# Output projection of a hybrid encoder layer: seven block products for eight, weight sums formed ahead, routing products set between dense ones

## What is computed

```python
h = rms_norm(x, norm1_g); proj = h @ w_in              # latents, z gate, delta-net inputs
mla_out = mla_mixer(...)                               # 8 heads of 128
gdn_out = gdn_mixer(...)                               # 8 heads of 128
x = x + jnp.concatenate([mla_out, gdn_out], axis=-1) @ w_o      # (768, 2048) @ (2048, 2048)
x = x + ec_moe(rms_norm(x, norm2_g), w_router, w_gate, w_up, w_down)
# ec_moe: affinities = softmax(xt @ w_router); each of the 16 experts takes its top
# 2*T/16 tokens of a set (32 of the prompt, 64 of the sample), SwiGLU of width 1024, added back
```

## Time and profile before

| | |
|---|---|
| median of 3 runs | 3069.76 us |
| profiled execution | 3071.65 us |
| its span (first to last instruction) | 3069.8 us |
| TensorE busy | 2891.6 us |
| mean granted TensorE clock | 0.976 of full |
| bytes moved | 561 MB, mean 183 GB/s |
| latents end / projection begins / last dense product ends / experts begin | 319.7 / 1625.2 / 1947.2 / 1966.6 us |

### The profile page before, as it was taken

One profiled execution on the slowest core, in us unless ns is written; L12 is line 12 of the kernel. 1 busy time (PEld: TensorE's weight loads), 2 busy tenths in 40 slices (PEclk: granted clock), 3 DMA queues, 4 the chain that ended last, 5 costly groups with the idle time before them and its releaser, 6 DMA issues. The chain is left out here.

```text
span 3069.8 us, 45507 instructions
## 1 busy us (share of the span) xinstructions
PE 2891.6 (94%) x19449; PEld 1451.7 (47%) x19449; DVE 890.9 (29%) x1613; ACT 512.7 (17%) x1333; POOL 409.8 (13%) x400
## 2 busy tenths in 40 slices
PE   8999999999999999998899999799999999999997
PEld 4544455555676666665564456333332232322232
DVE  1000344421764664675761022300000000000000
ACT  4110355412213213214111001100000000000000
POOL 0000111104114214215210000000110000011001
PEclk9999999999999999998999999899999999999998
DMA  5120200030211211103205113799999999999996
GB/s 184 55 73 21 68 28 28 11 118 28 56 53 38 56 42 49 56 15 118 72 22 212 55 55 155 289 404 397 386 390 381 395 395 394 393 394 387 391 396 250
DMA packets 140611, 561.01 MB, mean 183 GB/s; under 512 B 15216, under 2 KB 47816, under 8 KB 87240
## 3 DMA queue, kind: packets, MB, share of 16 engines
q1 hardware_dynamic: 131527, 534.08, 45.1%
q0 software_dynamic: 8960, 25.17, 3.9%
HBM read 524.25 MB, written 34.96 MB: 182 GB/s over the span
## 5 line engine op out<-in xcount | busy, mean ns | idle before, releaser
L2398 PE MATMUL psum<-wbuf,xeT 128*32 128x512 f32 x3120 | 356.8, 610 | 35.2 <-DMA wbuf<-in_w_up 32.3
L1222 PE MATMUL psum<-xT,wbuf 128*128 128x512 f32 x720 | 337.6, 606 | 0.3 <-PEq L612 0.3
L2398 PE MATMUL psum<-xT,xeT 128*32 128x512 f32 x3024 | 330.1, 592 | 0.0
L1992 PE MATMUL psum<-wbuf,xT 128*128 128x512 f32 x656 | 288.4, 601 | 1.0 <-PEq L1147 1.0
L460 PE MATMUL psum<-wbuf,xT 128*128 128x512 f32 (+1 forms) x704 | 281.1, 559 | 0.9 <-DVE xT L380 0.9
L2398 PEld LDWEIGHTS psum<-wbuf,xeT 128*32 128x32 f32 x3120 | 101.6, 113 | 283.6 <-issue 229.7
L2398 PEld LDWEIGHTS psum<-xT,xeT 128*32 128x32 f32 x3024 | 98.1, 110 | 226.4 <-issue 222.5
L1992 PEld LDWEIGHTS psum<-wbuf,xT 128*128 128x128 f32 x656 | 126.8, 195 | 157.6 <-issue 157.6
L460 PEld LDWEIGHTS psum<-wbuf,xT 128*128 128x128 f32 x704 | 133.4, 191 | 139.1 <-issue 120.0
L2481 DVE COPY hT<-psum 128x384 f32<-128x384 f32 x16 | 8.9, 557 | 646.9 <-PE psum L2381 646.9
L1222 PEld LDWEIGHTS psum<-xT,wbuf 128*128 128x128 f32 x720 | 132.1, 193 | 125.5 <-issue 120.5
(11 more groups left out here) (299 smaller groups left out, 3060.0 us busy)
## 6 DMA issues: line engine op xcount, KB each, us to landing
xT<-in_w_down SPq DMA_DIRECT2D x66, 1024.0 KB, 25.4
wbuf<-in_w_gate SPq DMA_DIRECT2D x65, 1024.0 KB, 20.1
wbuf<-in_w_up SPq DMA_DIRECT2D x65, 1024.0 KB, 23.5
xT<-in_w_gate SPq DMA_DIRECT2D x63, 1024.0 KB, 18.6
xT<-in_w_up SPq DMA_DIRECT2D x63, 1024.0 KB, 21.0
wbuf<-in_w_down SPq DMA_DIRECT2D x62, 1024.0 KB, 25.3
wbuf<-in_w_in SPq DMA_DIRECT2D x14, 2048.0 KB, 9.2
wbuf<-in_w_o SPq DMA_DIRECT2D x6, 4096.0 KB, 14.9
```

Source lines behind the costliest of these rows:

```text
L1222: last = nc.tensor.matmul(ps[:, b, 0:SS_], wg[:, m % 2, d, h * P:(h + 1) * P], k.xT[:, d, SP_:T], start=(d == 0), stop=(d == KD - 1))
L1992: last = nc.tensor.matmul(ps[:, u % 3, :], mixT[:, q, t * P:(t + 1) * P], wo[:, j % 2, q, :], start=(q == q0), stop=(q == 2 * H - 1))
L2398: last = nc.tensor.matmul(ps[32 * j:32 * j + 32, g, :].rearrange("p (x n) -> p x n", x=2), xeT[:, q, 32 * g:32 * g + 32], m[:, :, kk, 256 ...
```

## The change

**Seven products for eight.** The tiles are taken in pairs (even, odd) = (2, 3), (4, 5), (0, 1). The left matrix of a pair is [[E_l, E_h], [O_l, O_h]] (E and O: rows of the even and odd tile; l and h: heads 0 to 7 and 8 to 15), `w_o` is [[W_ll, W_lr], [W_hl, W_hr]] (low and high heads, left and right 1024 columns). With D = E_l - O_l, S2 = O_h - D, S1 = E_l + S2, S4 = E_h - S2 and the weight sums T1 = W_lr - W_ll, T3 = W_hr - W_lr, T2 = T3 + W_ll, N4 = W_hl - T2, seven products (p = 1: E_l W_ll, 2: E_h W_hl, 3: S4 W_hr, 4: O_h N4, 5: S1 T1, 6: S2 T2, 7: D T3), each of 8 heads for two halves j of 512 columns, give the four output blocks by additions. That is 3 x 7 x 2 x 8 = 336 products of 128 x 512 in place of 384. p = 1 and heads 0 to 6 of the first two units of p = 7 are made in deltanet.

**Weight sums in latents.** SP loads all four quarters of `w_o` in 32 steps of 128 partitions x 4 x 256 elements, VectorE combines each in three operations, and SP stores the four sums to `weight_sums`, 16 MB each way. 14 steps lie among the kv latents, 18 among the z slices.

**Routing between dense products.** A group of four transposes, or of four router products, follows each second dense product of a unit, in place of all 16 between two units.

```diff
@@ latents, SP @@
+                def comb_load(u):
+                    q, j, half = u // 4, (u // 2) % 2, u % 2
+                    if u >= 2:
+                        sp.wait_ge(s_cs[u % 2], 16 * (u // 2))
+                    c0 = 512 * j + 256 * half
+                    src = a["w_o"][0].rearrange("(g q p) (h c) -> g q p h c", g=2, p=P, h=2)[:, q, :, :, c0:c0 + 256]
+                    for g in range(2):
+                        sp.dma_start(comb[:, u % 2, 2 * g:2 * g + 2], src[g]).then_inc(s_cl[u % 2], 16)
+
+                def comb_store(lo, hi):
+                    for u in range(lo, hi):
+                        q, j, half = u // 4, (u // 2) % 2, u % 2
+                        c0 = 512 * q + 256 * half
+                        sp.wait_ge(s_comb, u + 1)
+                        sp.dma_start(k.wt[:, j, :, c0:c0 + 256].rearrange("m p c -> p m c"), comb[:, u % 2]).then_inc(s_cs[u % 2], 16)
+                        if 1 <= u < COMBOS - 1:
+                            comb_load(u + 1)
...
-                for g in range(1, 4):
-                    load_w(g)
+                load_w(1)
+                load_w(2)
+                comb_load(0)
+                comb_load(1)
+                comb_store(0, 11)
+                load_w(3)
                 sp.dma_start(k.wq[:], a["w_q_b"][0].rearrange("(p k) n -> p k n", k=4)[:, :, 0:2 * QH]).then_inc(k.s_wa, 16)
                 sp.dma_start(k.wkv[:], a["w_kv_b"][0].rearrange("(p k) n -> p k n", k=2)[:, :, 0:2 * (NOPE + VH)]).then_inc(k.s_wa, 16)
+                comb_store(11, 14)
                 sp.wait_ge(s_gv, 6)
...
+                    if half == 0:
+                        comb_store(14, 24)
+                    else:
+                        comb_store(24, COMBOS)
                     sp.wait_ge(s_z, NT * half + nt)
...
+                for x in range(2):
+                    sp.wait_ge(s_cs[x], 16 * COMBOS // 2)
@@ latents, VectorE @@
+                def combine(lo, hi):
+                    for u in range(lo, hi):
+                        w = comb[:, u % 2]
+                        dve.wait_ge(s_cl[u % 2], 32 * (u // 2 + 1))
+                        odd = w.rearrange("p (g h) c -> p g h c", h=2)[:, :, 1]
+                        st.done(nc.vector.tensor_tensor(w[:, 0:2], odd, w[:, 0:2], ALU.subtract))
+                        st.settle()
+                        st.done(nc.vector.tensor_tensor(w[:, 3], w[:, 3], w[:, 0], ALU.subtract))
+                        st.settle()
+                        nc.vector.tensor_tensor(w[:, 2], w[:, 2], w[:, 3], ALU.subtract).then_inc(s_comb, 1)
...
                 for u in range(NT - 1, 2 * NT):
                     store_latent(u)
+                    combine(2 * (u - NT + 1), 2 * (u - NT + 1) + 2)
...
                     nc.vector.tensor_tensor(o, o, bcast(gng[:], 1, 4), ALU.mult).then_inc(s_z, 1)
+                    if v < 9:
+                        combine(14 + 2 * v, 16 + 2 * v)
@@ deltanet, SP (last pair of heads) @@
+                        for j in range(2):
+                            sp.dma_start(k.slot[j], weight_half(a, 0, 0, j)).then_inc(k.s_wo[j], 16)
                         sp.wait_ge(s_out, i * 16)
                         sp.dma_start(k.mixT[:, H:2 * H - 2], k.mix[H:2 * H - 2].rearrange("h p t -> p h t")).then_inc(k.s_mix, 16)
-                        sp.dma_start(k.wo[:, 0], a["w_o"][0].rearrange("(k p) n -> p k n", p=P)[:, :, 0:512]).then_inc(k.s_wo[0], 16)
-                        sp.wait_ge(s_silu, HP * NC)
-                        for o, t in enumerate(PARTS):
-                            sp.dma_start(part[o], k.x_rows(t)[:, 0:512]).then_inc(s_px, 16)
...
-                for o in range(len(PARTS)):
+                sp.wait_ge(s_pp, N_PART)
+                sp.dma_start(k.slot[1], k.wt[T3, 1].rearrange("p (q n) -> p q n", q=H)).then_inc(k.s_wo[1], 16)
+                for o in range(N_PART):
                     sp.wait_ge(s_pa, o + 1)
                     sp.dma_start(k.part[o], part[o]).then_inc(s_out, 16)
@@ deltanet, GpSimd @@
+                        if r == 1 and i + 1 == HP:
+                            pool.wait_ge(k.s_mix, 32)
+                            for even, odd in PAIRS:
+                                o = k.mixT[:, 0:H, odd * P:(odd + 1) * P]
+                                nc.gpsimd.tensor_tensor(o, k.mixT[:, 0:H, even * P:(even + 1) * P], o, ALU.subtract).then_inc(s_convv, 1)
@@ output_and_route @@
-    ORDER = [2, 3, 4, 5, 0, 1]
+    ORDER = [3, 5, 2, 4, 0, 1]
+    PRODUCTS = [(p, j, i) for p in (7, 6, 5, 3, 4, 2) for j in range(2) for i in range(2)]
+    UNIT = [u // 2 for u in range(24)] + [10, 11] + list(range(12, 22))
+    PRODUCTS += [(p, j, 2) for p in (2, 6, 5, 3, 7, 4) for j in range(2)]
...
+    TURN = {20: 0, 21: 1, 24: 2, 25: 3, 33: 4}
+    ROUTE = {22: 0, 23: 1, 26: 2, 27: 3, 34: 4}
+    AFFINITY = {24: 0, 25: 1, 28: 2, 29: 3, 35: 4}
@@ output_and_route, SP @@
+                def load_w(v):
+                    u = UNIT.index(v)
+                    p, j, _ = PRODUCTS[u]
+                    if v >= 3:
+                        sp.wait_ge(s_acc, last_use[v - 3] + 1)
...
+                    sp.dma_start(k.slot[v % 3], src).then_inc(s_w[v % 3], 16)
...
+                sp.wait_ge(k.s_gdn, rows_to)
+                for t in ORDER[0:2]:
+                    sp.dma_start(x2[:, t, :], k.x_rows(t)).then_inc(k.s_gdn, 16)
+                load_w(2)
+                for t in ORDER[2:4]:
+                    sp.dma_start(x2[:, t, :], k.x_rows(t)).then_inc(s_x, 16)
+                sp.dma_start(part, k.part.rearrange("o p n -> p o n")).then_inc(k.s_mix, 16)
+                for t in ORDER[4:6]:
+                    sp.dma_start(x2[:, t, :], k.x_rows(t)).then_inc(s_x, 16)
...
+                for v in range(3, NV):
+                    load_w(v)
+                    if v == 12:
+                        rows_out(0)
+                        rows_out(1)
...
@@ output_and_route, TensorE @@
+                    for q in range(NEAR if u < 2 else 0, H):
...
+                        last = nc.tensor.matmul(ps[:, u % 3, :], left, k.slot[v % 3][:, q, :], start=(q == 0), stop=(q == H - 1))
...
+                        if q % 2 and u in TURN:
+                            transposes(TURN[u], q // 2)
+                        if q % 2 and u in ROUTE:
+                            router(ROUTE[u], q // 2)
+                        if q % 2 and q < H - 1 and u == NU - 1:
+                            last_transposes(q // 2)
```

More of the change, by code:

```diff
@@ L47, with weight_half @@
 SECOND = 8
-PARTS = (2, 3, 4, 5)
-PART_HEADS = 2 * H - 2
+PAIRS = ((2, 3), (4, 5), (0, 1))
+T1, T3, N4, T2 = range(4)
+COMBOS = 32
+N_PART = 6
+PART_STEPS = N_PART * H
+NEAR = H - 1
+def weight_half(a, low, right, j):
+    return a["w_o"][0].rearrange("(g q p) n -> g p q n", g=2, p=P)[low, :, :, 1024 * right + 512 * j:1024 * right + 512 * j + 512]
 def shape_constants():
@@ L167, in latents @@
     k.s_gdn = k.sem("deltanet_stored")
-    k.part = nc.dram_tensor("output_part", [len(PARTS), P, 512], F32).ap()
+    k.part = nc.dram_tensor("output_part", [N_PART, P, 512], F32).ap()
+    k.wt = nc.dram_tensor("weight_sums", [4, 2, P, H * 512], F32).ap()
+    k.slot = [k.wbuf[:, v // 2, H * (v % 2):H * (v % 2) + H, :] for v in range(4)]
     k.s_ring = [k.sem(f"unit_loaded{q}") for q in range(6)]
+    k.ring_base = [16 * COMBOS] * 2 + [8 * COMBOS] * 2 + [0] * 2
     k.s_act, k.act_steps = k.sem("scalar_step"), 0
@@ L1131, in deltanet @@
         s_vec = sem("deltanet_vector_step")
-        part = [(pre, y)[o // 3][:].rearrange("p b n -> p (b n)")[:, 512 * (o % 3):512 * (o % 3) + 512] for o in range(len(PARTS))]
+        part = [(pre, y)[o // 3][:].rearrange("p b n -> p (b n)")[:, 512 * (o % 3):512 * (o % 3) + 512] for o in range(N_PART)]
         w_d = a["w_in"][0].rearrange("(p k) n -> p k n", k=KD)
@@ L1760, in _ @@
                                 convolve(i + 1, 1, [lv + 1])
+                            if not more and r == 0 and lv == 5:
+                                copy_part(0)
+                            if not more and r == 1 and lv == LV:
+                                copy_part(2)
                         if r < 2:
@@ L1771, in _ @@
                     if not more:
-                        add_part(2)
+                        copy_part(5)
                     output(i)
-                    if not more:
-                        add_part(3)
                     if more:
@@ new lines, in transposes, with router @@
+                def transposes(o, b):
+                    if b == 0:
+                        pe.wait_ge(s_xn, o + 1)
+                    if o:
+                        pe.wait_ge((s_td, s_ta)[b % 2], 2 * o - 1 + b // 2)
+                    for j in range(4):
+                        m = 4 * b + j
+                        last = nc.tensor.transpose(ps[:, 3 + b, j * P:(j + 1) * P], xn[:, o % 2, m * P:(m + 1) * P], k.ident)
+                    last.then_inc(s_tp, 1)
+                def router(o, b):
```

(40 more changed lines are left out.)

296 lines of the change are left out of this document (162 added, 134 removed).

## The result

The changed kernel takes 3086.2 us (median of 4 runs, 3084.07 to 3087.41), the kernel before 3069.43 us beside it: ratio 1.0055, 95% interval 1.0042 to 1.0068. It is **slower by 17 us**; 3052 had been forecast, with a range of 3028 to 3076. The profiled execution took 3084.07 us; its span is 3082.3, 12.5 us more than the 3069.8 before.

The account below looks back on a forecast made before the run. The experts' weight stream sets their length, so time saved or lost before them counts in full. Projection -48.2, DeltaNet +0.7 and latents +30.3 sum to -17.2 us: 3052 us against the median 3069.76, range 3028 to 3076.

Parts of the forecast that it names:

- Weight sums in the latents: Latents: 32 load, combine, store steps form one serial chain; the stage ends at 350 against 319.7, +30 us.
- L: Period of one weight-sum step in the latents: 6.6 us, low bound 5.7, high bound 8.3.
- 185 + 25L: Time in us at which the latents end, given the sums' step period; 350 was forecast.
- detour behind step 10: Latents: SP issues z weights, wq and wkv (5.4 MB, 15 us), so step 12 comes 15.7 us after step 11.
- TensorE ahead of its cumulative sum: Latents: the cumulative sum, at 210.71 before, runs at 221, +10 us, behind VectorE's late gate arithmetic.
- Rival B: Latents: every load waits behind a store; slower from a period of 7.55 us, 3095 us at 8.3; chance 0.13.
- 25L - 182: Whole kernel's net change in us by the sums' step period; crosses zero at 7.3 us.
- Rival A: Latents: the sums hide, period 5.9 us or less; net -35 to -40, 3030 to 3035 us; chance 0.14.
- C: Projection: starved by weight loads of 12 us rather than 8; +26 us, net +9 or about -1; chance 0.06.
- D: Routing: the clock falls in spite of interleaving; +10 us, net -7, 3063 us; chance 0.08.
- Projection: Output projection with routing: products -46.3, routing -9.9, start +6, small waits +2; 321.8 to 273.6 us, -48.2.
- Routing: Projection: interleaving with dense products keeps the clock full, 38.0 to 28.1 us, -9.9; bounds 0 and -12.

Follow-up runs that it names:

- experiment 5: Changed kernel without the stores of the weight sums; combinations stay, the projection reads plain quarters of the weights: 3029.53 us.
- experiment 6: Changed kernel with each tile's four groups of transposes, or of router products, together behind a unit's last dense product: 3089.04 us.
- experiment 7: Kernel of experiment 6 with router products directly ahead of the next tile's transposes at three of four places: 3095.16 us, ratio 1.0084.
- experiment 2: Changed kernel with SP issuing the load of step u+1 ahead of its wait for step u's combination: 3040.88 us.
- experiment 3: Changed kernel with four buffers for the sums in place of two, three loads ahead: 3025.98 us.
- experiment 1: Changed kernel without the weight sums in the latents; the projection loads quarters of w_o of the same size instead: 3027.7 us.
- experiment 8: Four-buffer kernel with the projection's fourth and fifth weight loads issued ahead of router weights, gain and two late x tiles: 3013.74 us.

## Why the prediction was wrong, step by step

- **Weight sums in the latents: the step that failed**, in its term L. The mechanism was the forecast's: one serial chain, its three operations, SP's loads behind its stores. L was put at 6.6 us; it is 7.56. The term of the sum that was mis-sized is the moving of the store's and the load's 1.05 MB "behind each other at 350 GB/s, 3.0 us": the windows show 5.0 us, 1.5 for the store and 3.5 for the load. The 1.95 us put around it for first byte and completion are about 1.0, which hides half of the error. The load by itself was no surprise: without the store it costs 4.0 us from signal to landing (experiment 5), and the prediction's two bounds have 4.1 and 3.95 for it. It is the store ahead of it that adds 1.96, where 6.6 left 1.0.
- **Where the 350 GB/s came from**: a row that is mostly a 2 MB transfer. It held a warning: where its 1 MB store ends and the load begins stand three slices of 0.75 us at 243, 191 and 277 GB/s, 0.5 MB in some 2.2 us. The prediction took them for a dip of 0.5 us. To a load of 2 MB they are little, to one of 0.5 MB nearly all; that they are the same slowness as the 164 GB/s is likely, but not shown. That 2 MB load too is in 1 KB runs and reaches 392 GB/s later, so the length of the runs is not shown to be the cause. The figure worked out from the Trainium skill (DMA: Bandwidth & Descriptors, Anatomy of one DMA), 6.0 us, was further off still; the page fits it to single transfers that GpSimd issues, and these are SP's, one behind the other.
- The formula 185 + 25L gives 374 for 7.56; 381.6 was measured, so the size of L explains 24 of the 32 us that were missing. Of the other 7.6, 2.9 had been lost by step 10 (its store at 199.97, where 136.6 + 8L gives 197.1). The **detour behind step 10** has 3.6: SP is through with the weights' issues only at 212.06 (wq alone held it for 6.65 us), the store of step 11 waits behind them, and steps 10 to 12 take 26.0 us where the sum had 22.4. (It had put 6.6 for one L in that figure; with 7.56 it would be 23.3.) The rows of gates ahead of step 14 have 2.8 (steps 13 to 15 take 19.2 us, 16.4 in the sum), and the later steps gave some 2 back. In experiments 6 and 7 the stage ends some 3 us earlier, so the 7.6 is partly the execution's.
- **TensorE ahead of its cumulative sum**: it came 25.7 us later than before rather than 10, 15.4 past the forecast 221. Nine steps of a longer L make 8.6 of that; the rest is the 2.9 and 3.6 above and 0.3 of step 13.
- **Rival B** (longer chain, slower kernel) had 0.13 and is what happened, just past its threshold of 7.55. It had the place right, the load behind the store. The high bound's picture, a load that starts when the store has landed (8.3), is not what the windows show: the load's data follow the store's at once, and slowly. The range was said to reach L = 7.6 with 3076; by 25L - 182 that is 3078. Rival A's 5.9 is reached by other code only, and a period of 5.83 does not hide the sums yet (experiment 2, 17 us left); 3.7 does (experiment 3). C and D did not happen: no wait for weights recurs after the first, and the clock is 1.00 in the routing.
- **Projection**: 274.6 against 273.6. Products -46.3 by count (548 records). Routing -9.2 against -9.9, but half of it by a cause that the prediction had not named: the tables that part router and transposes (experiments 6, 7). That the sum fits so well is luck to that extent. The stretch ahead of routing has 137.7 - 296 x 0.429 = 10.7 us beyond its products, before 187.8 - 432 x 0.429 = 2.5: +8.2 against 6 + 2. The wait ended 36.7 us into the stage, was 6.94 long and was followed by 7 us at a clock of 0.56, some 3 us more, which fills the place of the "small waits".
- **DeltaNet** with attention: +2.6 against +0.7; nothing here says why. The experts are 4.9 us shorter (1096.7 from their first TensorE record, 1101.6 before); in experiments 1 to 3 and 6 to 8 they took 1097.7 to 1101.8 us with the same code, so a few microseconds of that stage vary with the execution, and no run has a cause for them.
- **Net**: 25L - 182 gives +7 us at 7.56; with the latents' other 7.6 it is +14.6. DeltaNet and the projection add 2.9 and the experts take 4.8 away: 12.7, and the spans differ by 12.5.

## What to carry to other kernels

Where an in-order queue waits for step u, stores it and only then loads u + 1, two buffers overlapped nothing here. Put the load ahead of the wait for the combination (one line moved: 45 us here), or add buffers until a load is free to go while the step before it is combined (58 us). Price such a chain with a transfer of its own size and in its own place, here the first half megabyte behind a store, not with the mean rate of a large one. If the verdict turns within a microsecond of its period, as here, the range must reach to the other side. Compare the new work with what it is to hide behind: at 3.7 us a step it fits into this stage, at 7.6 it sets the stage's length.

## What was not expected of the hardware

- With 48 small TensorE records in a row (32 router products, 16 transposes) at three places, the granted clock of that stretch was 0.90; with the two parted by dense records 0.96; in groups of four or eight between dense ones 1.00. The engine was busy all the time but for one wait of 1.64 us in the first.
- A TensorE wait of 6.9 us cost about 10: the products behind it ran at 0.56 for 7 us. (Taking out the 6.26 us wait of experiment 3 gave 9.6.)
- A 512 KB load in 1 KB runs moved at 260 GB/s alone and at 164 behind a 512 KB store.
- Issuing wq's load occupied SP for 6.65 us with the load of step 11 and 4 MB of z weights issued right before it, in place of 0.55 for the load of the same size at 405.93, in the attention. That the backlog is the reason is not tested.
